# Differential attention: value products behind the scores of three units ahead, in ScalarE's banks and copied out by ScalarE

## The chip, the cores and the metric

The kernel runs on one core of a Trainium2 chip. Its time is the time of one execution on the device in microseconds (us). TensorE (PE) multiplies matrices and writes to eight banks of PSUM; VectorE (DVE) and ScalarE (ACT) read those banks; GpSimd (POOL) and SyncE (SP) issue transfers here. Each engine works through its own list of instructions in order, and the engines wait for each other by semaphores.

## The reference

Two transformer blocks on 512 tokens of width 1024, in float32. The change is in one part of the first block, the differential attention: four heads, each with two sets of queries and keys of width 64 and values of width 128.

```python
def one_block(args):
    qb, blk = args
    ...
    logits = jnp.einsum('bhqmd,bhmkd->bhmqk', qb, k_t).astype(f32) * scale
    logits = logits + bias[None, :, None]
    logits = jnp.where(allowed[None, None, None], logits, NEG_INF)
    probs = jax.nn.softmax(logits, axis=-1)
    attn = (probs[:, :, 0] - lam * probs[:, :, 1]).astype(v_t.dtype)
    return jnp.einsum('bhqk,bhkd->bhqd', attn, v_t)
...
o = rms_norm(from_blocks(o), out_g) * (1.0 - lam_init)
```

After it come the output projection (`w_out`), the residual, and the norm ahead of the feed-forward part.

## The kernel before

**Units and turns.** The differential attention is cut into 16 units: unit n is head n % 4 of the 128 tokens of group q = n // 4. A unit of group q has scores over (q + 1) * 128 keys. Every engine runs the loop `for n in DIFF_TURNS`, 25 turns, and each turn holds steps of several units and groups. What one engine does in turn n, in this order:

- **TensorE** (line 1055): the value product of unit n - 1, `diff_values` (q + 1 pairs of 128x128 tiles); the two score products of unit n + 3, `diff_scores`; in turns 0 and 4 eight matmuls of the conditioning (`modulation_sums`, line 849), in 2 and 6 one of its products (`modulation`, line 860); the turning (transposes, line 804) of unit n's weights, `diff_turns`. Then the steps of a group at fixed distances: in turn 4q + 6 `out_turned(q)`, in 4q + 11 `x_turned(q)`, and in turns 4q + 7 and 4q + 8 `out_product(q, 0)` and `out_product(q, 1)`, 128x1024 by 1024x512 each. The helper `product` records all these products as line 738.
- **VectorE** (line 1932): `diff_score(n + 2)` (line 1794, two reads of a bank with bias and row maximum), `diff_share(n)` (lines 1804 to 1807, which makes the difference of the two softmaxes and signals `p_ready`), `out_added` (line 1825), the copy `diff_out(n - 1)` (line 1799), and by group: `out_squares(q)` in turn 4q + 4 (lines 1811, 1812, 1601), `out_normal(q)` in 4q + 5 (lines 1598, 1818, 1819), `x_squares(q)` in 4q + 9 (line 1828), `x_normal(q)` in 4q + 10 (line 1834).
- **ScalarE** (line 2596): two exponentials of unit n (line 2603), the copy of unit n - 1's turned weights to `pT` (line 2515, the helper `copy_out`), in turn 4q + 7 the copy of the turned output rows to `yT`, the conditioning's copy in turns 0 and 4, and `root` (line 2504, a square root): in turn 4q + 5 for `out_squares(q)`, in 4q + 10 for `x_squares(q)`. `root` and the exponentials need different tables, so that a `root` brings two table loads: one before it, one before the exponential that follows.

**Banks.** The eight banks are two rings of four. VectorE empties banks 0 to 3, ScalarE banks 4 to 7, each in the order in which TensorE filled them. `bank` makes TensorE wait until the fill four before it in the same ring was copied out. Before the change VectorE's ring holds a value product and two scores in each turn, ScalarE's ring the turned weights.

**What waits for what.** The turning of unit n waits for `diff_share(n)`, that for the exponentials of n; the value product of n waits for the copy of n's turned weights (`mark["diff", "T", n]`); `out_normal(q)` waits for ScalarE's `root`; `out_turned(q)` for `out_normal(q)`; `x_turned(q)` for `x_normal(q)`. `pT` has two buffers, `diff_s` has three pairs.

```python
def group_at(n, after):

    q, rest = divmod(n - 4 - after, 4)
    return q if rest == 0 and 0 <= q < NT else None
```

Of the kernel before, what the change touches and what calls it, by code (L numbers as in the profile page):

```python
# [24 lines left out]
P = 128  # L25
# [151 lines left out]
def build(nc, t, out):  # L177
# [6 lines left out]
    with ExitStack() as ctx:  # L184
# [109 lines left out]
        diff_o = S1["v"]  # L294
# [241 lines left out]
        n = len(items)  # L536
# [160 lines left out]
        def _(pe):  # L697
# [4 lines left out]
            def bank(ring_name):  # L702

                n = done[ring_name]
                free = dve_free if ring_name == "dve" else act_free
                if n >= 4:
                    pe.wait_ge(free, n - 3)
                last_share = last_shares.pop(n % 4 + (0 if ring_name == "dve" else 4), None)
                if last_share is not None:
                    pe.wait_ge(*fast_bank_free(last_share))  # L710
                return banks[n % 4 + (0 if ring_name == "dve" else 4)]
# [310 lines left out]

            def diff_values(n):
                h, q = diff_units[n]
                b = bank("dve")
                pe.wait_ge(act_free, mark["diff", "T", n])
                full(product(b[:, 0:P], [(S1["pT"][:, n % 2, k, 0:P], S1["dv"][:, k, h * P:(h + 1) * P])
                                         for k in range(q + 1)]), "dve")
                mark["diff", "PV", n] = done["dve"]

            def out_turned(q):
                to_wait(tp_ready)
# [20 lines left out]
            diff_scores(1)  # L1053
            diff_scores(2)
            for n in DIFF_TURNS:
                if 1 <= n <= N_DIFF:
                    diff_values(n - 1)
                diff_scores(n + 3)
                if n in (0, 4):
                    modulation_sums(10 + n // 4)  # L1060
                if n in (2, 6):
                    modulation(10 + n // 4)
                if n < N_DIFF:
                    diff_turns(n)
                q = group_at(n, 2)
                if q is not None:
                    out_turned(q)
                q = group_at(n, 7)
                if q is not None:
                    if q == NT - 1:  # L1070
                        pe.wait_ge(dve_free, mark["ffn turned", 1])
                        fast_product(0, shares=(0,))
                    x_turned(q)
                for c in range(2):
                    q = group_at(n, 3 + c)
                    if q is not None:
                        out_product(q, c)
# [486 lines left out]
        def _(dve):  # L1564
# [229 lines left out]
                    V(dve.tensor_tensor_reduce(diff_s[j][:, 0:w], take()[:, 0:w], diff_bias[:, h, 384 - q * P:512],  # L1794
                                               -DIFF_QK ** -0.5, -BIG, ALU.add, ALU.min, neg_max[:, j:j + 1]), dve_free)

            def diff_out(n):
                h, q = diff_units[n]
                V(dve.tensor_copy(diff_o[:, q, h * P:(h + 1) * P], take()[:, 0:P]), dve_free)

            def diff_share(n):
                w, j = (diff_units[n][1] + 1) * P, 2 * (n % 3)
                wait_next(e_ready, 2)
# [3 lines left out]
                V(stt(s0, s0, row_sum[:, j:j + 1], s1, ALU.mult, ALU.subtract), p_ready)  # L1807

            def out_squares(q):
                v = diff_o[:, q, :].rearrange("p (g d) -> p g d", g=4)  # L1810
                V(tt(out_square, v, v, ALU.mult))
                V(dve.tensor_reduce(stat8[:, 0:DIFF_H], out_square, AX.X, ALU.add))
                scale_var(stat8[:, 0:DIFF_H], P, EPS, var_ready)
# [118 lines left out]
            for n in DIFF_TURNS:  # L1932
                if n + 2 < N_DIFF:
                    diff_score(n + 2)
                if n in (3, 7):
                    modulation(10 + n // 4)
                if n < N_DIFF:
                    diff_share(n)
                q = group_at(n, 8)
                if q is not None:  # L1940
                    turned_in(q, column("ffn_norm_g"), hT=ffn_hT)
                for c in range(2):
                    q = group_at(n, 4 + c)
                    if q is not None:
                        out_added(q, c)
                if 1 <= n <= N_DIFF:
                    diff_out(n - 1)
                for after, stage in ((1, out_normal), (0, out_squares), (6, x_normal), (5, x_squares)):
                    q = group_at(n, after)
                    if q is not None:  # L1950
                        stage(q)
                if n == N_DIFF + 5:
                    weight_sum(0, 0)
                if n == N_DIFF + 7:
                    weight_sum(0, 1)
# [526 lines left out]
        def _(act):  # L2482
# [31 lines left out]
            def copy_out(dst, src):  # L2514
                C(act.activation(dst, src, ACT.Copy), act_free)  # L2515
# [80 lines left out]
            for n in DIFF_TURNS:  # L2596
# [7 lines left out]
                                         accum_out=row_sum[:, j:j + 1]), e_ready)  # L2604
                if 1 <= n <= N_DIFF:
                    q = diff_units[n - 1][1]
                    if n >= 3:
                        act.wait_ge(dve_full, mark["diff", "PV", n - 3])
                    copy_out(S1["pT"][:, (n - 1) % 2, 0:q + 1, 0:P],
                             take()[:, 0:(q + 1) * P].rearrange("p (a b) -> p a b", a=q + 1))  # L2610
                q = group_at(n, 3)
                if q is not None:
                    copy_out(S1["yT"][:, 4:8, q * P:(q + 1) * P], take()[:, :].rearrange("p (a b) -> p a b", a=4))
                if n in (0, 4):
                    modulation_part(10 + n // 4)
                if group_at(n, 1) is not None:
# [421 lines left out]
```

## Time and profile before

| | |
|---|---|
| time, three runs | median 2320.02 us (2319.14 to 2322.25) |
| the profiled execution | 2320.72 us, span 2318.9 us |
| PE busy over the span | 2122.4 us (92%) |
| DVE busy | 1203.8 us (52%) |
| ACT busy | 439.4 us (19%) |
| differential attention, the 16 units with copies and norms | about 276 to 380 us of the span |

Times in the rows below count from the start of the span, in microseconds. In a timeline a row is a run of instructions of one line: its start, its length, what it is, how many, and in square brackets the idle time of the engine ahead of it and who ended it.

### The profile page before, as it was taken

What the parts mean: (1) busy time and instruction counts of PE and PEld (TensorE: products, weight loads), DVE (VectorE), ACT (ScalarE), POOL (GpSimd) and SP (SyncE); (2) the same over time, 40 slices, a digit from 0 to 9 for tenths busy, and PEclk for the clock granted to TensorE, in tenths of its full rate; (3) what the DMA queues carried; (4) which work ended last, traced back from release to release, by engine and by line L of the source; (5) the groups of instructions that cost most, each with busy time, mean ns of one, the idle gap of its engine ahead of it and who ended that gap; (6) DMA issues with size and microseconds to landing.
All of it is one profiled execution on the core that took longest, in us unless ns stands there. A gap on an engine that the chain in (4) does not pass through costs nothing.

```text
span 2318.9 us, 24664 instructions
## 1 busy us (share of the span) xinstructions
PE 2122.4 (92%) x9190; PEld 1351.5 (58%) x9190; DVE 1203.8 (52%) x2145; ACT 439.4 (19%) x901; POOL 125.1 (5%) x159
## 2 busy tenths in 40 slices
PE   7998788999999999998899999999996999999882
PEld 3444444888888844434688488888854333433330
DVE  4684563756676533287688357776446212121114
ACT  1124442100100010104311354510110000000003
POOL 0000000000000000000000044300000001010000
PEclk9998988999999999999999999999996999999986
DMA  7126510522222121221032100042443899999994
GB/s 276 37 86 241 190 48 1 153 75 74 72 100 100 66 86 73 73 73 37 1 109 73 37 1 1 2 145 73 146 184 130 367 427 426 427 426 426 427 423 183
DMA packets 97293, 364.71 MB, mean 157 GB/s; under 512 B 10396, under 2 KB 19281, under 8 KB 84625
## 3 DMA queue, kind: packets, MB, share of 16 engines
q1 hardware_dynamic: 86337, 340.62, 38.2%
q0 software_dynamic: 8720, 20.89, 2.4%
q8 instruction: 76, 1.25, 0.2%
q10 hardware_dynamic: 2112, 1.57, 0.2%
q14 instruction: 48, 0.39, 0.1%
HBM read 357.00 MB, written 17.57 MB: 162 GB/s over the span
## 4 chain that ended last, share of the span: by engine, by line
PE 74%; DVE 13%; DMA 7%; issue 3%; ACT 2%; SPq 0%; DVEq 0%; ACTq 0%; POOL 0%; POOLq 0%
PE bank L738 49%; PE bank L1527 8%; PE bank L1522 5%; DMA mem<-in_w_up 5%; PE bank L804 3%; PE bank L1217 2%; PE bank L974 2%; DVE mem L2103 1%; PE bank L849 1%; DVE mem L2102 1%; ACT mem L2515 1%; DMA mem<-in_w_in 1%; PE bank L1503 1%; DVE mem L1761 1%; PE bank L1157 1%
## 5 line engine op out<-in xcount | busy, mean ns | idle before, releaser
L738 PE MATMUL bank<-mem 128*128 128x256 f32 (+7 forms) x5024 | 1358.5, 432 | 31.8 <-ACT mem L2515 12.8
L738 PEld LDWEIGHTS bank<-mem 128*128 128x128 f32 (+2 forms) x5024 | 936.2, 193 | 404.8 <-issue 262.2
L1527 PE MATMUL bank<-mem 128*64 128x512 f32 x1248 | 287.3, 616 | 29.2 <-DMA mem<-in_w_up 16.6
L1527 PEld LDWEIGHTS bank<-mem 128*64 128x64 f32 x1248 | 93.1, 141 | 213.6 <-issue 202.2
L2515 ACT ACTIVATE mem<-bank 128x512 f32<-128x512 f32 (+5 forms) x269 | 136.8, 508 | 370.1 <-PE bank L738 153.1
L804 PE MATMUL bank<-mem 128*128 128x128 f32 (+1 forms) x708 | 118.8, 300 | 50.5 <-DVE mem L1761 24.6
L2451 DVE TENSOR_TENSOR mem<-mem,bank 128x512 f32<-128x512 f32 x19 | 13.1, 690 | 279.6 <-PE bank L1527 207.2
L804 PEld LDWEIGHTS bank<-mem 128*128 128x128 f32 (+1 forms) x708 | 88.1, 151 | 102.2 <-DVE mem L1761 37.6
L1522 PE MATMUL bank<-mem 128*128 128x512 f32 x288 | 132.3, 615 | 6.7 <-ACT mem L2797 4.1
L2628 ACT ACTIVATE mem<-bank 128x512 f32<-128x512 f32 (+1 forms) x62 | 36.3, 586 | 458.5 <-PE bank L738 456.8
L1522 PEld LDWEIGHTS bank<-mem 128*128 128x128 f32 x288 | 55.3, 196 | 78.7 <-issue 70.2
L2459 DVE TENSOR_TENSOR mem<-bank,mem 128x512 f32<-128x512 f32 x38 | 26.4, 693 | 106.1 <-PE bank L1527 71.3
L1217 PE MATMUL bank<-mem 128*128 128x128 f32 x512 | 64.1, 278 | 6.7 <-DVE mem L2243 5.0
L1847 DVE TENSOR_TENSOR mem<-mem 128x1024 f32<-128x1024 f32 (+2 forms) x31 | 36.4, 1175 | 62.5 <-PE bank L738 52.4
L1217 PEld LDWEIGHTS bank<-mem 128*128 128x128 f32 x512 | 59.9, 191 | 8.8 <-DVE mem L2243 6.0
L2795 ACT ACTIVATE mem<-bank 128x512 f32<-128x512 f32 x19 | 11.4, 599 | 262.7 <-PE bank L1527 191.4
L2165 DVE SCALAR_TENSOR_TENSOR mem<-mem 128x511 f32<-128x511 f32 (+2 forms) x72 | 54.1, 752 | 2.5
L2797 ACT ACTIVATE mem<-bank 128x512 f32<-128x512 f32 x19 | 11.4, 599 | 182.1 <-PE bank L1543 182.1
L974 PE MATMUL bank<-mem 128*64 128x512 f32 (+7 forms) x128 | 39.7, 454 | 3.1 <-ACT mem L2515 3.1
L1912 DVE TENSOR_TENSOR mem<-mem,bank 128x512 f32<-128x512 f32 (+1 forms) x30 | 20.2, 672 | 42.8 <-PE bank L738 42.4
L1892 DVE TENSOR_TENSOR mem<-mem,bank 128x512 f32<-128x512 f32 (+1 forms) x31 | 20.9, 673 | 39.3 <-PE bank L738 39.1
L1753 DVE CUSTOM_DVE_ANT_0 mem<-bank,mem 128x128 f32<-128x128 f32 (+1 forms) x64 | 31.5, 493 | 16.7 <-PE bank L738 14.8
(347 smaller groups left out, 1698.1 us busy)
## 6 DMA issues: line engine op xcount, KB each, us to landing
mem<-in_w_gate SPq DMA_DIRECT2D x37, 2048.0 KB, 23.3
mem<-in_w_up SPq DMA_DIRECT2D x37, 2048.0 KB, 23.5
mem<-in_w_down SPq DMA_DIRECT2D x36, 2048.0 KB, 22.5
mem<-in_w_in SPq DMA_DIRECT2D x18, 2048.0 KB, 7.7
mem<-in_w_ada SPq DMA_DIRECT2D x12, 2048.0 KB, 8.0
mem<-in_w_out SPq DMA_DIRECT2D x4, 2048.0 KB, 13.3
mem<-in_w_ple_gate SPq DMA_DIRECT2D x2, 2048.0 KB, 7.9
mem<-in_w_br_att SPq DMA_DIRECT2D x2, 2048.0 KB, 7.9
```

The source lines that it names most:

```text
L738: last = pe.matmul(o, l, r, start=(i == 0), stop=(i == len(pairs) - 1))
L804: last = pe.transpose(b[0:width, i * P:(i + 1) * P], s, ident)
L974: last = pe.matmul(o[:, k * P:SEQ], v_of(k, h), pT[:, h % nbuf, k, k * P:SEQ], start=(k == 0), stop=(k == NT - 1))
L1217: last = pe.matmul(b[:, h * P:(h + 1) * P], lhs(h), rhs(h), start=True, stop=True)
L1522: last_ = pe.matmul(o, lhs[:, k, :], ws[0][:, k, cols], start=(k == 0), stop=(k == kk - 1))
L1527: last_ = pe.matmul(o[here, :], lhs[:, k, here], w[:, k, cols], start=(k == 0), stop=(k == kk - 1))
L1753: V(dve.tensor_tensor_reduce(s[:, n % 3, 0:w], b[:, 0:w], bias_of(q), -scale, -BIG, ALU.add, ALU.min, neg_max[:, n % 4:n % 4 + 1]), dve_free)
L1847: V(tt(s1, feature_half(w, 0, 1), feature_half(w, 1, 1), ALU.add), w_summed)
L2165: V(stt(o, src[:, 0:SEQ - back], column("conv_w_2", (CONV2 - 1 - back) * 24 + m), o, ALU.mult, ALU.add), silu_in if back == CONV2 - 1 else ...
L2459: tt(yb[:, n % 2, at_], banks[5 + half][:, :], gate_rows[:, 1, at_], ALU.mult).then_inc(y_taken, 1)
L2515: C(act.activation(dst, src, ACT.Copy), act_free)
L2628: C(act.activation(dst[:, 0:cols], fast_bank(n, 3 * i)[:, 0:cols], ACT.Copy), fast_copied)
```

## The change

The value product of unit n - 1 goes to a bank of ScalarE's ring, not VectorE's. ScalarE copies it out, after the copies of turned weights and rows of the same turn and ahead of the conditioning's copy and `root`; VectorE's copy `diff_out` is gone. On TensorE the value product stands behind the score products of unit n + 3. `out_squares(q)` waits on ScalarE's copy of the group's last unit. ScalarE's wait for a free half of `pT` goes, since its own copy of the value product stands for it.

```diff
             def diff_values(n):
                 h, q = diff_units[n]
-                b = bank("dve")
+                b = bank("act")
                 pe.wait_ge(act_free, mark["diff", "T", n])
                 full(product(b[:, 0:P], [(S1["pT"][:, n % 2, k, 0:P], S1["dv"][:, k, h * P:(h + 1) * P])
-                                         for k in range(q + 1)]), "dve")
-                mark["diff", "PV", n] = done["dve"]
+                                         for k in range(q + 1)]), "act")
+                mark["diff", "PV", n] = done["act"]
...
             for n in DIFF_TURNS:
+                diff_scores(n + 3)
                 if 1 <= n <= N_DIFF:
                     diff_values(n - 1)
-                diff_scores(n + 3)
...
-            def diff_out(n):
-                h, q = diff_units[n]
-                V(dve.tensor_copy(diff_o[:, q, h * P:(h + 1) * P], take()[:, 0:P]), dve_free)
-
...
             def out_squares(q):
+                dve.wait_ge(act_free, mark["diff", "PV", 4 * q + 3])
                 v = diff_o[:, q, :].rearrange("p (g d) -> p g d", g=4)
...
-                if 1 <= n <= N_DIFF:
-                    diff_out(n - 1)
...
                 if 1 <= n <= N_DIFF:
                     q = diff_units[n - 1][1]
-                    if n >= 3:
-                        act.wait_ge(dve_full, mark["diff", "PV", n - 3])
                     copy_out(S1["pT"][:, (n - 1) % 2, 0:q + 1, 0:P],
                              take()[:, 0:(q + 1) * P].rearrange("p (a b) -> p a b", a=q + 1))
                 q = group_at(n, 3)
                 if q is not None:
                     copy_out(S1["yT"][:, 4:8, q * P:(q + 1) * P], take()[:, :].rearrange("p (a b) -> p a b", a=4))
+                if 1 <= n <= N_DIFF:
+                    h, q = diff_units[n - 1]
+                    copy_out(diff_o[:, q, h * P:(h + 1) * P], take()[:, 0:P])
                 if n in (0, 4):
                     modulation_part(10 + n // 4)
                 if group_at(n, 1) is not None:
```

On ScalarE, turns 9 and 10 (the exponentials of units 9 and 10, the copies of turned weights, the square roots) before:

```order
L2603 ACTIVATE mem<-mem 128x384 x2
L2515 ACTIVATE mem<-bank5 128x3x128
L2504 ACT_TABLE_LOAD
L2504 ACTIVATE mem<-mem 128x4
L2603 ACT_TABLE_LOAD
L2603 ACTIVATE mem<-mem 128x384 x2
L2515 ACTIVATE mem<-bank6 128x3x128
L2504 ACT_TABLE_LOAD
L2504 ACTIVATE mem<-mem 128x1
```

and after:

```order
L2598 ACTIVATE mem<-mem 128x384 x2
L2510 ACTIVATE mem<-bank5 128x3x128
L2510 ACTIVATE mem<-bank6 128x128
L2499 ACT_TABLE_LOAD
L2499 ACTIVATE mem<-mem 128x4
L2598 ACT_TABLE_LOAD
L2598 ACTIVATE mem<-mem 128x384 x2
L2510 ACTIVATE mem<-bank7 128x3x128
L2510 ACTIVATE mem<-bank4 128x128
L2499 ACT_TABLE_LOAD
L2499 ACTIVATE mem<-mem 128x1
```

The new rows are the two 128x128 copies from banks 6 and 4. Each stands between the copy of the turned weights and the table load of the square root.

On TensorE, turns 8 to 10 (x8 is an output product; 128x128 x3 of line 738 a value product with three tiles; two 128x512 a pair of scores; line 804 turned weights, and with x4 turned rows) before:

```order
L738 MATMUL bank1<-mem 128x512 x8
L738 MATMUL bank2<-mem 128x128 x3
L738 MATMUL bank3<-mem 128x512
L738 MATMUL bank0<-mem 128x512
L804 MATMUL bank6<-mem 128x128 x3
L738 MATMUL bank1<-mem 128x128 x3
L738 MATMUL bank2<-mem 128x512
L738 MATMUL bank3<-mem 128x512
L804 MATMUL bank7<-mem 128x128 x3
L804 MATMUL bank4<-mem 128x128 x4
```

and after:

```order
L738 MATMUL bank1<-mem 128x512 x8
L738 MATMUL bank2<-mem 128x512
L738 MATMUL bank3<-mem 128x512
L738 MATMUL bank6<-mem 128x128 x3
L804 MATMUL bank7<-mem 128x128 x3
L738 MATMUL bank0<-mem 128x512
L738 MATMUL bank1<-mem 128x512
L738 MATMUL bank4<-mem 128x128 x3
L804 MATMUL bank5<-mem 128x128 x3
L804 MATMUL bank6<-mem 128x128 x4
```

The value products moved from behind the output product and the turned weights to behind the pair of scores, and from banks 2 and 1 to banks 6 and 4. The output product of a turn still stands ahead of the value product of the next.

## Rows read from the trace of the kernel before

**Rows 1.** Page, part 4: the chain that ended last.
```profile
PE 74%; DVE 13%; DMA 7%; issue 3%; ACT 2%; SPq 0%; DVEq 0%; ACTq 0%; POOL 0%; POOLq 0%
```

**Rows 2.** Groups by line and form, 276 to 380 us.
```profile
L2504 ACT ACT_TABLE_LOAD x6 | 7.7, 1283 | 15.5 <-DVE mem L1601 15.5
...
L1799 DVE COPY mem<-bank 128x128 f32<-128x128 f32 x16 | 4.7, 293 | 2.7 <-PE bank L738 2.3
...
L2515 ACT ACTIVATE mem<-bank 128x128 f32<-128x128 f32 x4 | 1.1, 280 | 3.6 <-PE bank L804 3.6
```

**Rows 3.** Waits, 276 to 385 us: total, times, longest.
```profile
PE bank L738 <- ACT mem L2515: 10.2, 9, 2.2
```

**Rows 4.** Timeline of PE, turns 4 to 7.
```profile
293.76 2.77 PE L738 MATMUL bank<-mem 128*128 128x128 f32 x8 [2.19 <-ACT mem L2515]
...
298.24 2.78 PE L738 MATMUL bank<-mem 128*128 128x128 f32 x8 [1.09 <-ACT mem L2515]
...
299.37 1.65 PE L738 MATMUL bank<-mem 64*128 64x384 f32 x4
...
306.71 0.44 PE L804 MATMUL bank<-mem 128*128 128x128 f32 x2 [1.00 <-DVE mem L1807]
```

**Rows 5.** Timeline of ACT, turn 5 and 6.
```profile
293.63 1.28 ACT L2504 ACT_TABLE_LOAD   x1
...
296.45 0.51 ACT L2603 ACTIVATE mem<-mem 128x256 f32<-128x256 f32 x1
...
297.71 0.39 ACT L2515 ACTIVATE mem<-bank 128x256 f32<-128x256 f32 x1
```

**Rows 6.** Timeline of ACT, turns 9 to 11.
```profile
316.92 1.28 ACT L2504 ACT_TABLE_LOAD   x1 [0.51 <-DVE mem L1601]
...
327.01 1.28 ACT L2504 ACT_TABLE_LOAD   x1 [1.51 <-DVE mem L1601]
...
331.30 1.13 ACT L2515 ACTIVATE mem<-bank 128x384 f32<-128x384 f32 x2
```

**Rows 7.** Timeline of PE, turns 9 to 11.
```profile
324.34 0.55 PE L804 MATMUL bank<-mem 128*128 128x128 f32 x3
325.64 3.20 PE L738 MATMUL bank<-mem 128*128 128x128 f32 x10 [0.76 <-ACT mem L2515]
329.83 0.98 PE L804 MATMUL bank<-mem 128*128 128x128 f32 x7 [0.99 <-DVE mem L1807]
...
335.50 2.56 PE L804 MATMUL bank<-mem 128*128 128x128 f32 x11
```

**Rows 8.** Timeline of DVE, turns 9 and 10.
```profile
323.84 0.18 DVE L1598 RECIPROCAL mem<-mem 128x4 f32<-128x4 f32 x1
...
329.16 0.62 DVE L1807 SCALAR_TENSOR_TENSOR mem<-mem 128x384 f32<-128x384 f32 x1
```

**Rows 9.** Timeline of PE, turns 14 and 15.
```profile
356.33 1.13 PE L738 MATMUL bank<-mem 128*128 128x128 f32 x8 [0.86 <-ACT mem L2515]
360.18 1.97 PE L804 MATMUL bank<-mem 128*128 128x128 f32 x8 [2.73 <-DVE mem L1807]
363.88 2.05 PE L738 MATMUL bank<-mem 128*128 128x128 f32 x8 [1.73 <-ACT mem L2515]
365.72 2.77 PE L804 MATMUL bank<-mem 128*128 128x128 f32 x12
```

**Rows 10.** Timeline of ACT, turns 13 to 15.
```profile
347.99 1.28 ACT L2504 ACT_TABLE_LOAD   x1
...
358.63 1.28 ACT L2504 ACT_TABLE_LOAD   x1 [2.45 <-DVE mem L1601]
...
363.13 1.24 ACT L2515 ACTIVATE mem<-bank 128x512 f32<-128x512 f32 x2
```

**Rows 11.** Windows: length, busy time of each engine, then the granted clock (PEclk).
```profile
293.50:303.70 10.20, 8.85 (x25) 4.76 (x26) 5.37 (x15) 5.81 (x14) 0.00 (x0) 0.50 0.49 188
...
358.40:368.60 10.20, 6.69 (x29) 6.32 (x30) 5.30 (x13) 6.21 (x10) 0.00 (x0) 0.50 0.01 2
```

## The prediction

> **What bounds the kernel now.** I read the chain that ended last first: PE holds 74% of it [rows 1], so time is won where TensorE waits or runs at its lower clock. Then the waits of the stage: ahead of value products TensorE waited 10.2 us for ScalarE's copies, nine times, 2.2 us at most [rows 3]. That is what the scores could fill. Then the timelines of the three engines side by side. They show two kinds of turns. In turns 7 and 8, 11 and 12, 15 and 16 an output product of about 7 us stands on TensorE and VectorE and ScalarE have time in plenty. In the turns between, every engine waits for another in a ring: turned weights, ScalarE's copy, value product, and beside them the norms of a finished group, with ScalarE's square root. Last the windows for the clock: TensorE is granted half (1.2 GHz of 2.4) from 293.5 to 303.7 and 358.4 to 368.6 [rows 11], after waits of 2.19 us [rows 4] and of 0.86 us and more [rows 9].
>
> **The copies themselves.** 16 copies of 128x128 leave VectorE, 0.293 us each, and come to ScalarE at 0.280 us [rows 2]: 4.7 us against 4.5 us of busy time, no gain by itself. What decides is where the new copy stands in ScalarE's list. It waits for the value product of its unit, and behind it are queued the square root of the turn, the two exponentials of the next unit and the copy of the next turned weights; VectorE's norms and shares wait for these, and TensorE for the shares.
>
> **Turns 1 to 7, a gain.** A pair of scores fills the wait for ScalarE's copy of the turned weights, so up to turn 4 TensorE comes about 0.7 us sooner (an estimate: some 0.5 us in turn 4, where the scores now run while ScalarE copies, and 0.2 us brought along; the nine waits of [rows 3] are 1.1 us in the mean, but half of such a gain is lost again where the share of the turn is late). Then turn 5. The copy of unit 4's weights ended at 293.62 and its square root started at 293.63 [rows 5], while the value product had its start at 293.76 [rows 4]. With 0.7 us gained that product starts at 293.05; it takes some 0.8 us at the full clock, and ScalarE's copy another 0.1 + 0.28 us. The square root starts at 294.2, later by 0.6 us. From a square root to the end of the copy behind the next exponentials ScalarE's work is a solid row (293.63 to 298.10, [rows 5]), so value product 5 starts at 298.85, not 298.24 [rows 4]. But the scores of 1.65 us that followed it [rows 4] have been done before, so that turned weights 6 come 1.65 - 0.6 = 1.0 us sooner. From there to turned weights 7 at 306.71 [rows 4] VectorE's chain decides, as before. Term: **-1.0 us**. Bounds: if the shorter wait ahead of turn 5 keeps the full clock, what lies there takes about half as long, -2.5 us; if instead the longer wait ahead of value product 5 costs it further on, 0.
>
> **Turns 9 to 11, a loss.** Output product (0, 1) occupies TensorE until 322.5. Under it ScalarE did the square root of group 1 at 316.92 [rows 6]. Now the copy of unit 8 stands ahead of that root, and value product 8 stands behind the output product and the scores: it ends at about 324.4, just ahead of the turned weights of 324.34 [rows 7]. The root's table load starts at 324.4 + 0.1 + 0.28 = 324.8, later by 7.9 us, and nothing covers it. Load and root (1.28 + 0.2 us, [rows 2]) end at 326.3, VectorE's `out_normal(1)` starts there and not at 323.84, and so all of VectorE behind it, to the share of unit 10 that ended at 329.78 [rows 8], comes 2.5 us later: turned weights 10 at 332.3, not 329.83 [rows 7]. ScalarE goes on: from table load to the end of the next pair of exponentials took 331.30 - 327.01 = 4.29 us [rows 6], so the copy of weights 9 (0.49 us) ends at 324.8 + 4.3 + 0.5 = 329.6, value product 9 starts at 329.75 where it was 325.64 [rows 7]. Its wait is now over 3 us, so I take the lower clock: by the 1.13 us for two tiles (299.37 - 298.24, [rows 4]) three take 1.6 us. Its copy ends at 331.7, the second root (`x_squares(0)`) and its exponentials at 336.0, the copy at 336.5, value product 10 at 336.65 to 338.2. Behind it turned weights 11, at 335.50 before [rows 7]: **+2.7 us**. At the full clock the two value products are 0.7 to 0.8 us shorter each: +1.3 us.
>
> **Turns 13 to 15, the same once more.** The root of group 2 was at 347.99 [rows 10], under output product (1, 1). Now it follows the copy of unit 12, whose value product ends at 355.0. The copy ends at 355.4, root and exponentials at 359.9 (363.13 - 358.63 = 4.5 us, [rows 10]), the copy of weights 13 (0.60) at 360.5. Value product 13 starts at 360.65 instead of 356.33, takes 2.05 us at the lower clock (1.13 at the full one, [rows 9]), its copy ends at 363.1, root of `x_squares(1)` and exponentials of unit 15 at 367.6, the copy at 368.2, value product 14 at 368.35 instead of 363.88. Turned weights 15 follow 365.72 - 363.88 = 1.84 us behind [rows 9], at 370.2 instead of 365.72: **+4.5 us**. Both were at the lower clock in this stretch before [rows 11], and there is more waiting now, so I see no way back to the full clock; with it the term would be +2.6 us.
>
> **The clock behind.** Before, the full clock came back just as an output product began (303.7 and 368.6). I add **+0.7 us** for output products that now begin in a lower-clock stretch, an estimate: 1.4 us at half speed lose that in work. Bounds 0 and 3.
>
> **What costs nothing.** The wait of `out_squares(q)` for ScalarE's copy adds some 0.1 us and is under output products (turns 8, 12, 16) or behind a copy long done (turn 4). In turns 9 and 13 the exponentials of the unit come up to 7 us later than before, under the output product of turn 8 or 12, before VectorE's share is asked for; with that cover gone they would cost their 1.5 to 1.7 us. Turn 17's root has only `out_squares(3)` ahead and output product (2, 1) over it. TensorE's waits for banks get no longer: scores alone now reuse VectorE's banks, and four fills back in ScalarE's ring lie two units. Behind the stage TensorE's list of products starts later by what has been lost, as do the loads that it releases.
>
> **Sum:** -1.0 + 2.7 + 4.5 + 0.7 = +6.9 us. The profiled execution, 2320.72 us (its span 2318.9 us), would be 2327.6; it is 0.7 us above the median, and against that I predict 2320.0 + 6.9, about 2327 us. Three runs lay 3.1 us apart, and 0.2%, 4.6 us, is about what can be told from no change.
>
> **A page against the rows.** The root with its two table loads took 296.45 - 293.63 = 2.82 us here [rows 5]. The Trainium skill, ScalarE: Activation LUTs, section "What ACT_TABLE_LOAD costs", gives 1283 ns for the load, which the rows have too, but a drain on top, 2.66 us for every switch. By it the root that comes onto the path would cost 2.5 us more in each of the two places, and the sum would be about +12 us (2332). The rows show the load followed by the next instruction at once, so the sum goes by them.
>
> **Rivals.** (a) *No measurable change*: the same mechanism, with TensorE at its full clock in turns 9 to 15: -2.5 + 1.3 + 2.6 + 0 = +1.4 us, 2321.5, and up to +4.6 where only one stretch is spared. For it: idle times below 1.2 us left the clock alone at 325.64 [rows 7]. Against it: the new waits are 3 and 5 us. Chance 0.30. (b) *Faster*: the roots are not late enough to matter, and the scores' cover is all that is left: -1.0 to -2.5 us in turns 1 to 7, 0.76 and 0.86 us of waits filled or kept [rows 7, 9], and less lower clock, some -5 us, 2315. It decides at the place of value product 8: VectorE wants the root at 323.84, 1.5 us behind its start, so its copy would have to end by 322.3, and that is still inside the output product. Chance 0.07. (c) *The new ring in every turn*: value product, copy, exponentials, copy of weights, on ScalarE's side without a gap: in group 3 about 1.1 to 2.05 + 0.4 + 1.7 + 0.7 = 4 to 5 us a turn. Where turns were shorter (1 to 6) it would cost up to 1 us each, +12 us in all, 2332. Against it: these turns have narrow units with 1 us of exponentials. Chance 0.08. My forecast: 0.55.
>
> **Numbers.** Slower by over 0.2% takes (c) and most of the forecast, 0.62; within 0.2% takes (a) and a little of the forecast, 0.31; faster 0.07. The range, 2320.5 to 2332, leaves out (b) and the far end of (c).
>
> **What would show it.** In the profile after: ScalarE's table load of turn 9 behind a 128x128 copy and behind output product (0, 1), 7 to 8 us later against its surroundings; VectorE idle ahead of the reciprocal of `out_normal(1)` and `(2)`, for ScalarE, some 2.5 and 1.5 us; waits of TensorE of 3 to 5 us ahead of value products 9 and 13, and turned weights 15 about 6 us later than 365.72; turned weights 7 ahead of 306.71. Wrong it would be if the lower-clock stretches end sooner or fewer come, or if the gain of the first seven turns is several times as large.

## The result, and the profile after

The changed kernel took 2334.11 us in the median of six runs (2328.49 to 2335.99), the kernel before beside it 2321.22 us (six runs, 2319.14 to 2324.14): ratio 1.0055 [1.0042, 1.0067]. It is slower by 12.9 us, and 2334 lies outside my range of 2320.5 to 2332. A second set of runs (e1 below) gave 10.6 us. One execution of the experiments (the profiled one of e10) ran at a granted clock of 0.55 and took 3702 us; its time and trace are left out.

The profiled execution took 2335.23 us, span 2333.4. Page of the kernel after, parts 1 and 4 (answers to [rows 1]):

```profile
PE 2132.6 (91%) x9190; PEld 1358.1 (58%) x9190; DVE 1198.9 (51%) x2129; ACT 443.8 (19%) x917; POOL 124.4 (5%) x159
...
PE 74%; DVE 12%; DMA 7%; issue 3%; ACT 2%; SPq 0%; DVEq 0%; ACTq 0%; POOL 0%; POOLq 0%
```

The copies moved as forecast (VectorE 4.9 us less, ScalarE 4.4 us more), and the chain hardly differs. But PE is busy for 2132.6 us, not 2122.4: the same 9190 matmuls took 10 us longer. That is the clock, not a wait, and not all of it is the change's: this execution had 13 us more at the lower clock ahead of the stage, where nothing was changed, and 11 us more behind it. In a second trace of the same kernel (e1) PE is busy for 2120.4 us. A page alone can't say what the change did.

Now the place in question. Waits of the kernel after, 282 to 391 us (total, times, longest), answering to [rows 3]:

```profile
ACT mem L2510 <- PE bank L738: 50.4, 16, 8.4
...
PE bank L738 <- ACT mem L2510: 21.2, 9, 5.2
...
DVE mem L1598 <- ACT mem L2499: 11.3, 5, 3.1
```

TensorE's nine waits for ScalarE's copies grew from 10.2 us to 21.2 (longest 5.2, was 2.2). ScalarE waits sixteen times for a value product, up to 8.4 us, and VectorE's reciprocal 3.1 us for ScalarE's root. The timelines of the kernel after show how. ScalarE, turns 9, 10 and 13 ([rows 6, 10] before):

```profile
331.59 0.28 ACT L2510 ACTIVATE mem<-bank 128x128 f32<-128x128 f32 x1 [6.85 <-PE bank L738]
331.89 1.28 ACT L2499 ACT_TABLE_LOAD   x1
...
334.70 0.62 ACT L2598 ACTIVATE mem<-mem 128x384 f32<-128x384 f32 x1
...
343.12 1.13 ACT L2510 ACTIVATE mem<-bank 128x384 f32<-128x384 f32 x2
...
363.46 0.28 ACT L2510 ACTIVATE mem<-bank 128x128 f32<-128x128 f32 x1 [5.60 <-PE bank L738]
363.76 1.28 ACT L2499 ACT_TABLE_LOAD   x1
```

VectorE, turn 9 ([rows 8] before):

```profile
333.49 0.18 DVE L1598 RECIPROCAL mem<-mem 128x4 f32<-128x4 f32 x1 [3.12 <-ACT mem L2499]
...
338.80 0.62 DVE L1803 SCALAR_TENSOR_TENSOR mem<-mem 128x384 f32<-128x384 f32 x1
```

TensorE, turns 5 to 7, 9 to 12 and 14 to 15 ([rows 4, 7, 9] before):

```profile
302.04 0.68 PE L738 MATMUL bank<-mem 128*128 128x128 f32 x4 [1.35 <-ACT mem L2510]
...
307.72 0.68 PE L738 MATMUL bank<-mem 128*128 128x128 f32 x4 [3.67 <-ACT mem L2510]
...
313.55 0.44 PE L804 MATMUL bank<-mem 128*128 128x128 f32 x2 [0.51 <-DVE mem L1803]
...
331.75 1.13 PE L738 MATMUL bank<-mem 64*128 64x512 f32 x4
336.82 1.62 PE L738 MATMUL bank<-mem 128*128 128x128 f32 x6 [3.94 <-ACT mem L2510]
339.48 1.76 PE L804 MATMUL bank<-mem 128*128 128x128 f32 x7 [1.04 <-DVE mem L1803]
...
344.59 1.42 PE L804 MATMUL bank<-mem 128*128 128x128 f32 x11
...
346.11 9.04 PE L738 MATMUL bank<-mem 128*128 128x512 f32 x26
...
369.01 2.05 PE L738 MATMUL bank<-mem 128*128 128x128 f32 x8 [5.21 <-ACT mem L2510]
...
376.70 1.96 PE L738 MATMUL bank<-mem 128*128 128x128 f32 x8 [3.94 <-ACT mem L2510]
378.45 2.34 PE L804 MATMUL bank<-mem 128*128 128x128 f32 x12
```

The signs that the prediction named are there: ScalarE sat 6.85 us in front of the copy of value product 8, its table load right behind; then VectorE's 3.12 us, and 3.94 and 5.21 us ahead of value products 9 and 13. Counted from each kernel's first score read, the table load of turn 9 came at 331.89 - 280.55 = 51.3 us, before at 316.92 - 274.54 = 42.4: 9.0 us later, where 7 to 8 were forecast. One sign is missing: turned weights 7 came no sooner (they stand under "Why" below).

**Three segments.** Starts differ between executions, so I cut each trace at the same four events: the first score read of the stage (VectorE, line 1794), the last addition of an output product (`out_added(3, 1)`), the first matmul of the experts (TensorE, line 1522 in both kernels), and the end. "Half clock" is the time at the lower granted level, 1.2 GHz. These are differences of start times in the timelines, in us:

```
run                 start   stage  half clock | behind  half clock | rest
before, 1st        274.5   130.9    34.1      | 1388.4    63.4     | 525.0
before, 2nd (e5)   275.9   130.9    34.1      | 1387.7    62.8     | 522.0
before, 3rd (e6)   275.2   130.7    30.7      | 1387.4    62.4     | 522.5
before, 4th (e17)  272.8   133.4    38.2      | 1388.0    63.3     | 521.2
before, 5th (e18)  280.0   130.7    30.7      | 1388.3    63.3     | 525.2
after, 1st         280.6   136.8    34.8      | 1392.6    74.6     | 523.5
after, 2nd (e1)    278.0   136.8    34.8      | 1393.0    75.1     | 525.2
after, 3rd (e11)   274.9   137.7    37.5      | 1392.1    74.0     | 524.4
```

The stage costs 5.9 us (twice; 6.8 once), near the +6.9 of the sum. Another 4 to 5 us come in 1390 us of program behind the stage that the change does not touch. The start is a drift of executions: it varies over 7 us in the kernel before alone, so the 6 us of it in the first pair of profiles can't be put down to the change (means 275.7 us in five traces of before, 277.8 in three of after).

Windows of both kernels over the part behind (length, busy time of PE, PEld, DVE, ACT, POOL, granted clock, DMA share, GB/s). After, then one of its stretches at half clock:

```profile
417.40:1810.00 1392.60, 1329.07 (x6131) 997.72 (x6129) 862.48 (x1416) 271.82 (x555) 77.84 (x109) 0.97 0.23 77
...
1141.40:1148.20 6.80, 5.38 (x12) 2.90 (x10) 0.12 (x1) 0.60 (x1) 0.00 (x0) 0.50 0.00 0
```

Before, then its stretch at the same distance from the stage's end (1141.40 - 417.36 = 1129.50 - 405.45 = 724.0 us):

```profile
405.40:1794.00 1388.60, 1325.09 (x6131) 994.67 (x6129) 862.71 (x1416) 271.85 (x555) 77.96 (x109) 0.98 0.23 78
...
1129.50:1136.30 6.80, 4.71 (x20) 3.32 (x21) 2.68 (x4) 1.09 (x2) 0.00 (x0) 1.00 0.00 0
```

The same 6131 matmuls; DVE and ACT are busy alike to 0.3 us, PE 4.0 us longer. The eight matmuls of line 974 that stand in the second stretch, the kernel after:

```profile
1143.02 4.61 PE L974 MATMUL bank<-mem 128*128 128x512 f32 x8 [0.84 <-ACT mem L2510]
```

and the kernel before:

```profile
1131.39 2.39 PE L974 MATMUL bank<-mem 128*128 128x512 f32 x8 [0.84 <-ACT mem L2515]
```

The wait ahead of them is 0.84 us in both; only the clock differs.

### The profile page after: what moved, and what is told of

It reads as the page before. It is cut to its first block, busy times and chain, and to the rows that moved or that the text cites. A ratio compares the mean times of both kernels' runs of the same rounds, so it can differ in the third digit from the quotient of the medians.

```text
span 2333.4 us, 24668 instructions
## 1 busy us (share of the span) xinstructions
PE 2132.6 (91%) x9190; PEld 1358.1 (58%) x9190; DVE 1198.9 (51%) x2129; ACT 443.8 (19%) x917; POOL 124.4 (5%) x159
## 4 chain that ended last, share of the span: by engine, by line
PE 74%; DVE 12%; DMA 7%; issue 3%; ACT 2%; SPq 0%; DVEq 0%; ACTq 0%; POOL 0%; POOLq 0%
PE bank L738 49%; PE bank L1527 8%; PE bank L1522 5%; DMA mem<-in_w_up 5%; PE bank L804 3%; PE bank L1217 2%; PE bank L974 2%; PE bank L849 1%; DVE mem L2098 1%; DVE mem L2097 1%; ACT mem L2510 1%; PE bank L1503 1%; DMA mem<-in_w_in 1%; PE bank L1157 1%; DVE mem L1761 1%
## 5 line engine op out<-in xcount | busy, mean ns | idle before, releaser
L738 PE MATMUL bank<-mem 128*128 128x256 f32 (+7 forms) x5024 | 1362.9, 433 | 42.4 <-ACT mem L2510 23.8
L2510 ACT ACTIVATE mem<-bank 128x512 f32<-128x512 f32 (+6 forms) x285 | 141.2, 496 | 391.0 <-PE bank L738 202.7
L974 PE MATMUL bank<-mem 128*64 128x512 f32 (+7 forms) x128 | 42.4, 479 | 3.1 <-ACT mem L2510 3.1
L1909 DVE TENSOR_TENSOR mem<-mem,bank 128x512 f32<-128x512 f32 (+1 forms) x30 | 20.2, 672 | 45.2 <-PE bank L738 44.8
L1598 DVE RECIPROCAL mem<-mem 128x8 f32<-128x8 f32 (+2 forms) x39 | 7.2, 184 | 66.0 <-ACT mem L2499 59.8
## 6 DMA issues: line engine op xcount, KB each, us to landing
mem<-in_w_up SPq DMA_DIRECT2D x37, 2048.0 KB, 24.6
```

The lines of the kernel that those rows point to most:

```text
L738: last = pe.matmul(o, l, r, start=(i == 0), stop=(i == len(pairs) - 1))
L974: last = pe.matmul(o[:, k * P:SEQ], v_of(k, h), pT[:, h % nbuf, k, k * P:SEQ], start=(k == 0), stop=(k == NT - 1))
```

## The experiments

**e1, e5, e6, e11, e17, e18: both kernels again.** No edit.

> The changed kernel once more, unaltered. Its first profile began the stage (first score product of differential attention) at 279.6 us against 273.6 before, 6.0 us late ahead of anything that the change touches, and was 5.9 us longer inside the stage and 2.6 us behind it. Theory M: only what lies inside the stage is the change's (square roots behind the new copy), the rest is the drift of one execution, so that the stage is again 5 to 7 us longer while its start lies anywhere from 273 to 280; time +6 to +13 us. Rival N: the changed program is slower outside the stage too, and the start is at 279 to 280 again, time +12 to +14 us.

> The kernel before, unaltered, for a second trace of it. The five traces of changed kernels began the stage 1.0 to 6.0 us later than the one trace of before, although the program ahead of it is the same, and TensorE's lower-clock stretches lay elsewhere. Drift theory: this trace begins the stage 1 to 6 us later than 274.5 us too, and its stage (first score to the last output product) may be a few us off 130.9. Theory N (the change slows the program outside the stage): it begins at 274.5 again. Time within 0.2% of before either way.

> The kernel before, unaltered, for a third trace, with the same two expectations as for the second: the drift theory has the start of the stage and the places of the lower clock vary between the traces of one kernel, theory N has them as in the first.

> The changed kernel, unaltered, for a third trace: the stage 5.9 us longer than before as in both others (6.9 predicted for it), the start between 274 and 281 us.

> The kernel before, unaltered, a fourth trace. If the start of the stage is the drift of an execution, at least one of this and the next begins it later than 276.5 us; if an altered program begins later by itself, both lie at 274.5 to 276. The stage 130.7 to 130.9 us, the stretch from its last output product to the experts 1387.4 to 1388.4 us, unless the later start brings the other pattern of the clock (1391.6 us and more).

> The kernel before, unaltered, a fifth trace, with the same expectations as the fourth.

Measured: after 2333.41 (six runs) against 2322.79, ratio 1.0044 [1.0028, 1.0060], and one run of 2330.94; before 2323.02 against 2323.95 (ratio 1.0008 [0.9991, 1.0026]), and single runs of 2317.57, 2317.21 and 2326.04. The traces gave the table above. Stage and part behind repeat within about 1 us for each kernel, except one stage of 133.4; the start does not repeat. The fifth trace of before began its stage at 280.0 us and still had 1388.3 us behind it: a late start does not bring the longer part behind.

**e2, e8: the roots ahead of the copy.** The cause of the loss should be ScalarE's order. e2 puts both `root`s ahead of the new copy, e8 only that of the output norm.

```diff
+                if group_at(n, 1) is not None:
+                    root(stat8[:, 0:DIFF_H])
+                q = group_at(n, 6)
+                if q is not None:
+                    root(stat[:, q:q + 1])
                 if 1 <= n <= N_DIFF:
                     h, q = diff_units[n - 1]
                     copy_out(diff_o[:, q, h * P:(h + 1) * P], take()[:, 0:P])
                 if n in (0, 4):
                     modulation_part(10 + n // 4)
-                if group_at(n, 1) is not None:
-                    root(stat8[:, 0:DIFF_H])
-                q = group_at(n, 6)
-                if q is not None:
-                    root(stat[:, q:q + 1])
```

(e8 leaves the second of the two where it was.)

> The changed kernel with one edit: in each turn ScalarE does its square roots ahead of the copy of the value product, not behind it. Only the next turn's exponentials and copy of turned weights still wait behind the copy. Theory M: VectorE's norms of groups 1 and 2 have their root under the output product again, the stage is 1 to 3 us longer than before in place of 5.9, time +1 to +4 us. Rival (the copy's wait itself, ahead of the exponentials, is the cost): the stage stays 5 to 7 us longer, time +6 or more. Rival N: start of the stage at 279 to 280, 6 us on top of either.

> The changed kernel with only the square root of the output norm (turns 5, 9, 13, 17) ahead of the copy; the square root of the feed-forward norm (turns 10, 14) stays behind it. With both ahead the stage went from +5.9 to -0.9 us. If the output norm's root is what came late, this one has most of that: stage 0 to +2 us, time +2 to +5 us. If the feed-forward norm's root carries it, the stage stays at +4 us or more.

Measured, e2: 2326.86 (twelve runs), ratio 1.0016 [1.0005, 1.0027], stage 129.97, 6.8 us less than after. ScalarE:

```profile
329.06 0.28 ACT L2510 ACTIVATE mem<-bank 128x128 f32<-128x128 f32 x1 [5.33 <-PE bank L738]
329.36 1.28 ACT L2598 ACT_TABLE_LOAD   x1
```

VectorE and TensorE of e2:

```profile
327.87 0.18 DVE L1598 RECIPROCAL mem<-mem 128x4 f32<-128x4 f32 x1
```

```profile
332.77 0.91 PE L738 MATMUL bank<-mem 128*128 128x128 f32 x6 [2.42 <-ACT mem L2510]
```

The copy still waits 5.33 us, but the root is no longer behind it: the reciprocal has no wait, and value product 9 waits 2.42 us, not 3.94. e8: 2329.43, ratio 1.0025 [1.0012, 1.0039], stage 134.52, 2.3 us less. So moving the output norm's root gave 2.3 us, about a third of the 6.8, and moving the feed-forward norm's root as well the other two thirds (the second move alone was not run). The order on ScalarE is the cause in the stage; what of the 6.8 us is wait and what is clock is not separated (24.6 us of e2's stage are at half clock, 34.8 of after's). e2's stage had been expected 1 to 3 us longer than before and came out 0.9 us shorter; e8's, 3.6 us longer, is nearer to the 4 us that had been expected if the feed-forward norm's root carried the loss than to the 0 to 2 us of the other case. Yet e2, with the shorter stage, stays slower than before: behind it are 1393.2 us.

**e3, e12: the copy a turn later.** ScalarE copies value product n - 2 right behind the exponentials of unit n, when it is long done; nothing has to wait for it.

```diff
+                if 2 <= n <= N_DIFF + 1:
+                    h, q = diff_units[n - 2]
+                    copy_out(diff_o[:, q, h * P:(h + 1) * P], take()[:, 0:P])
+                if n == 0 or n == 5:
+                    modulation_part(10 + n // 5)
                 if 1 <= n <= N_DIFF:
                     q = diff_units[n - 1][1]
                     copy_out(S1["pT"][:, (n - 1) % 2, 0:q + 1, 0:P],
...
-                if 1 <= n <= N_DIFF:
-                    h, q = diff_units[n - 1]
-                    copy_out(diff_o[:, q, h * P:(h + 1) * P], take()[:, 0:P])
-                if n in (0, 4):
-                    modulation_part(10 + n // 4)
```

> The changed kernel with ScalarE's copy of a value product one turn later, behind the next unit's exponentials (and the conditioning's copy behind it, as the ring wants), so that neither root nor exponentials ever wait for a value product. Theory M: nothing of the loss is left, the scores still fill TensorE's waits: the stage is 1 to 4 us shorter than before, time -1 to -4 us. Rival (ScalarE's 16 more copies, or the value product behind the scores, cost in themselves): the stage is 2 us or more longer than before. Rival N: time 6 us above what the stage says.

> The version with ScalarE's copy one turn later once more, for a second trace and more times: its stage 4 to 5 us shorter than before again; if it beats both kernels, time -1 to -4 us with an interval below 1.

Measured: 2321.05, ratio 0.9993 [0.9981, 1.0005], and 2319.92, ratio 0.9988 [0.9979, 0.9998], twelve runs each. The stage takes 126.2 and 124.2 us, 4.7 and 6.7 less than before. TensorE in e3:

```profile
326.83 2.00 PE L738 MATMUL bank<-mem 64*128 64x512 f32 x10
331.47 0.98 PE L804 MATMUL bank<-mem 128*128 128x128 f32 x7 [2.65 <-DVE mem L1803]
...
333.89 0.91 PE L738 MATMUL bank<-mem 128*128 128x128 f32 x6 [0.38 <-ACT mem L2510]
```

The ten matmuls are the scores and value product 8 together, and value product 9 waits 0.38 us. This is what the cover of the scores can give. Behind it come 1393.9 and 1393.3 us, and most is lost again: e3's interval includes no change, and e12's ends just below it.

**e4, e7: the value product in its old place,** ahead of the scores, in the changed kernel (e4) and in e3's (e7).

```diff
             for n in DIFF_TURNS:
-                diff_scores(n + 3)
                 if 1 <= n <= N_DIFF:
                     diff_values(n - 1)
+                diff_scores(n + 3)
```

> The changed kernel with the value product ahead of the scores again, as before; ScalarE's ring and copy stay. Theory M: each value product ends one pair of scores (0.6 to 1.1 us) sooner and with it the roots behind it, but the scores no longer fill waits: stage 4 to 6 us longer than before, time +4 to +8 us. Rival (the place behind the scores is what costs): stage within 1.5 us of before, time within 2 us.

> ScalarE's copy one turn later, behind the next exponentials, and the value product ahead of the scores as before. Theory R (the place behind the scores was worth 7.4 us under the late wait, 5.9 against 13.3 us of stage, because it alone gives TensorE work while ScalarE waits): with nothing waiting on ScalarE it is worth what the filled waits are, 2 to 5 us; the stage is 0 to 3 us shorter than before, time 0 to -2 us. Rival (the place is worth 7 us whatever stands behind the copy): stage 2 us or more longer than before.

Measured: e4 2337.30, ratio 1.0060 [1.0038, 1.0082], stage 144.25, 7.4 us more than after and 13.3 more than before, far more than I expected of it. e7 2326.02, ratio 1.0006 [0.9994, 1.0018], stage 127.97, 1.8 and 3.7 us above e3 and e12. TensorE in e4, where I had expected a short wait ahead of a value product:

```profile
335.47 3.50 PE L738 MATMUL bank<-mem 128*128 128x128 f32 x10 [3.79 <-ACT mem L2510]
```

e7's stage is 2.9 us shorter than before, as expected, but its time is not: 1391.6 us lie behind it. So the place behind the scores is a gain in both, largest while the copy makes everybody late; what makes the stage slow is where the copy stands. And e4 has 1388.4 us behind its stage, the value of before, though its program there is the changed kernel's.

**e9, e10, e13 to e16: a delay at the stage's end.** Is it the moment at which the stage ends that costs the 4 to 5 us behind? The kernel before, with N unused multiplies on VectorE in `out_normal(3)`; nothing else changes.

```diff
             def out_normal(q):
                 v = diff_o[:, q, :].rearrange("p (g d) -> p g d", g=4)
                 invert(stat8[:, 0:DIFF_H])
+                if q == NT - 1:
+                    for _ in range(8):
+                        V(tt(out_square, v, v, ALU.mult))
```

> The kernel before with nothing of the change, but with eight further multiplies of 128x512 (0.73 us each, 5.8 us in all) on VectorE in turn 17, ahead of the last group's output norm, where TensorE waits for it. Their result is used by nobody. It shifts all that follows by about what the change costs inside the stage. Theory P (what was lost outside the stage is TensorE's clock, which falls at other places once the same program runs at another time): behind the last output product 2 us or more are lost beside the three traces of before, time +9 to +14 us. Rival (the loss outside comes from the changed program itself): behind it within 1 us of them, time +6 to +8 us.

> The same with four multiplies, 2.9 us. Theory P: behind the last output product the loss is some value between -1 and +5 us that need not be the one with eight, time +3 to +8 us. Rival: within 1 us of before behind it, time +3 to +4 us.

> The kernel before with one further multiply (0.73 us) in turn 17, its result unused. If the moment decides, lower-clock time between 900 and 1900 us may be anything from 58 to 75 us and the time from the last output product to the experts goes with it (0 at 58 to 65, +3 to +5 at 72 to 75). If the changed program decides, it is 58 to 65 and within 1 us of before.

> The same with two multiplies, 1.5 us. If the moment decides, at least one of the four delays has 70 us or more of lower clock behind the stage and 3 us or more of extra time; if the changed program decides, none has.

> The same with three multiplies, 2.2 us, and the same two expectations.

> The same with six multiplies, 4.4 us, and the same two expectations.

The eight multiplies in e9 and the wait behind them, VectorE and TensorE:

```profile
392.90 5.79 DVE L1820 TENSOR_TENSOR mem<-mem 128x512 f32<-128x512 f32 x8
```

```profile
400.20 1.12 PE L804 MATMUL bank<-mem 128*128 128x128 f32 x4 [8.35 <-DVE mem L1822]
```

Measured: e9 2332.74, ratio 1.0044 [1.0031, 1.0057]; e10 2330.71 (six runs), ratio 1.0035 [1.0023, 1.0047], no trace; e13, e14, e15, e16 one run each, 2325.34, 2326.49, 2328.96, 2335.42 beside 2319.51. The part behind, by the traces, with the runs of the other kernels:

```
run                        stage  | behind  half clock
before + 1 multiply (e13)  131.2  | 1391.8    73.9
before + 2 (e14)           136.5  | 1388.7    62.7
before + 3 (e15)           136.3  | 1388.4    63.1
before + 6 (e16)           138.0  | 1391.6    73.9
before + 8 (e9)            140.3  | 1388.7    59.7
value product's place (e4) 144.3  | 1388.4    63.2
roots first (e2)           130.0  | 1393.2    75.2
one root first (e8)        134.5  | 1391.7    73.9
late copy (e3)             126.2  | 1393.9    75.6
late copy again (e12)      124.2  | 1393.3    75.4
late, old place (e7)       128.0  | 1391.6    73.7
```

The same work takes either 1387.4 to 1388.7 us with 60 to 63 us at half clock, or 1391.6 to 1393.9 us with 74 to 76; there is nothing between. One multiply of 0.7 us, which lengthened the stage by 0.3 us, brought the kernel before into the second group; two, three and eight left it in the first, though they lengthened the stage by 5 to 9 us; with six it is in the second again. In e9 the part behind came out as the rival of its expectation had it (within 1 us of before); the 2 us or more that Theory P wanted came in e13 and e16 alone. So neither the move of the copy nor a longer stage makes the 4 us. In the window of e13 (columns as above):

```profile
1137.00:1141.00 4.00, 3.71 (x8) 2.02 (x6) 0.19 (x1) 0.00 (x0) 0.00 (x0) 0.50 0.00 0
```

e13 is the kernel before, and it has the stretch at half clock that the kernel before lacks (there 1129.5 to 1136.3 was at 1.00) and the kernel after has.

The moment at which the stage ends does not sort the traces either. Counted from the start of the span, stages end at 405.5, 405.9 and 406.7 us (before, first group) and at 405.8 (e7, second); at 410.7 (before, e18, first) and at 410.3 (e13) and 410.5 (e8, second); at 416.9 (e15, first) and at 417.4 (e16, second). What repeats is the kernel: before fell in the first group five times of five, after in the second three times of three, the late copy (e3, e12) in the second twice. Programs that differ by one unused multiply can differ in the group.

One thing ahead of 724 us also goes by the kernel. In all five traces of before VectorE starts a reciprocal, about 679 us behind the stage's end, after an idle 0.37 us that no wait in the profile explains, and TensorE waits 0.41 us for what follows. In the other 14 traces the two idle times are at most 0.04 and 0.12 us, in e13 too. Before:

```profile
1084.13 0.16 DVE L1760 RECIPROCAL mem<-mem 128x1 f32<-128x1 f32 x1 [0.37 <-DVE mem L1753]
```

```profile
1084.87 0.66 PE L804 MATMUL bank<-mem 128*128 128x128 f32 x4 [0.41 <-DVE mem L1761]
```

and e13:

```profile
1088.35 0.16 DVE L1760 RECIPROCAL mem<-mem 128x1 f32<-128x1 f32 x1
```

```profile
1089.09 0.66 PE L804 MATMUL bank<-mem 128*128 128x128 f32 x4
```

Ahead of 724 us it is the only one of TensorE's idle times that separates the five traces of before from the ten of the second group by 0.25 us or more; across it the ten gain about 0.35 us. That this pause decides on the clock at 724 us is not shown.

## Why the prediction was right and wrong

**The copies themselves, and ScalarE's queue: right.** 4.9 us left VectorE and 4.4 came to ScalarE, and e2 shows that the order on ScalarE is the cause of the stage's loss. VectorE's waits for the root were 3.1 and 2.1 us, forecast some 2.5 and 1.5.

**The stage: +5.9 us where the sum had +6.9, in part by luck.** All times are from each trace's first score read, in us; the forecast column adds up the terms of the sum.

```
                     forecast | before  after  measured
turned weights 7       -1.0   |  32.2    33.0   +0.8
turned weights 11      +1.7   |  61.0    64.0   +3.1
turned weights 15      +6.2   |  91.2    97.9   +6.7
end of the stage       +6.9   | 130.9   136.8   +5.9
```

Term by term: +0.8 for -1.0, +2.3 for +2.7, +3.6 for +4.5, -0.8 for +0.7. The mechanism of the two losses was right and each a little smaller than forecast; the gain ahead of them did not come, and the clock term had the wrong sign. These misses cancel but for 1 us.

- *Turns 1 to 7, -1.0: the gain did not come.* Turned weights 7 started at 313.55 - 280.55 = 33.0 us, before at 306.71 - 274.54 = 32.2 [rows 4]: +0.8, and against three of the other traces of before (e5, e6, e18) it is +0.1 to +0.3. The scores did gain up to turn 5, as I had it. A second trace of before (e5) has value product 4 at 298.21 - 275.87 = 22.3 us, the kernel after at 302.04 - 280.55 = 21.5, 0.85 us sooner. Then it went: value product 5 waited 3.67 us for ScalarE, and the scores no longer behind it were worth 0.9 us at the full clock, where I had taken 1.65 us from a row at the lower one. [Rows 4] lay in a lower-clock stretch that other executions of the same kernel have elsewhere. TensorE in e5, where the product and the scores together take 1.53 us:

```profile
298.21 2.78 PE L738 MATMUL bank<-mem 128*128 128x128 f32 x8 [2.19 <-ACT mem L2515]
...
302.69 1.53 PE L738 MATMUL bank<-mem 128*128 128x128 f32 x8 [1.09 <-ACT mem L2515]
...
308.75 0.44 PE L804 MATMUL bank<-mem 128*128 128x128 f32 x2 [0.99 <-DVE mem L1807]
```

- *Turns 9 to 11, +2.7 forecast, +2.3 measured, and 13 to 15, +4.5 and +3.6.* Turned weights 11 (the row of eleven on line 804) started at 344.59 - 280.55 = 64.0, before at 335.50 - 274.54 = 61.0 [rows 7]. Those eleven took 1.42 us at the full clock, before 2.56 us, so that the row of 26 matmuls with output product (1, 0) began only 2.2 us later than before (346.11 - 280.55 = 65.6, and 337.89 - 274.54 = 63.4 by the row below). Turned weights 15 started at 378.45 - 280.55 = 97.9 against 365.72 - 274.54 = 91.2 [rows 9]. Value product 13 was at the lower clock as forecast (2.05 us), value product 9 too (1.62 us, forecast 1.6); value product 10, forecast 1.5 to 1.6 us as well, was back at the full clock (0.91 us). The kernel after, then before:

```profile
343.76 0.91 PE L738 MATMUL bank<-mem 128*128 128x128 f32 x6 [0.75 <-ACT mem L2510]
```

```profile
337.89 8.77 PE L738 MATMUL bank<-mem 128*128 128x512 f32 x26
```

- *The clock behind turn 15, +0.7: it was -0.8, outside its bounds of 0 and 3.* From turned weights 15 to the end of the stage the kernel before had 368.6 - 365.7 = 2.9 us left of one stretch at half clock and another from 385.7 to 392.5; the kernel after had 376.8 to 380.2, of which 1.8 us lay there, and 400.7 to 404.1.

**The step that failed is the sentence "Behind the stage TensorE's list of products starts later by what has been lost".** It took 1390 us of unchanged work for a constant. They cost 4 to 5 us more (1392.1 to 1393.0 against 1387.4 to 1388.4), 11 to 13 us more of them at half clock. With the 5.9 to 6.8 us of the stage this makes 10 to 12 us, against 12.9 and 10.6 in the medians; the rest is in the start and end, which vary by more than that. With the part behind as in the first group, the same stage would have given about 2321.2 + 5.9 = 2327 us (an estimate), inside the range, and e4 shows that a program with ScalarE's copy can be in that group. What the delays show is that this amount is not the work of the moved copy: the kernel before pays it too after one extra multiply. It repeats with each kernel and does not go by the moment at which the stage ends. What is not shown is why these kernels fall into two groups. Up to 670 us behind the stage all five traces of the kernel before and all ten of the second group have their stretches at half clock at the same distance from the stage's end, within 0.6 us; they part at 724 us, where the ten have one of 6.8 us more (after: 1141.4 - 417.4 = 724.0), and another of 3.4 us at 1024 us. The other four of the first group (e4, e9, e14, e15) have other arrangements, with a stretch of 10.2 us at 721 to 722 us, and nearly the same total. Why the clock parts there stays open, and with it whether the pause of 0.37 us has a part in it.

**The page against the rows.** By the Trainium skill's ScalarE: Activation LUTs, section "What ACT_TABLE_LOAD costs", the sum would have been about +12 us (an estimate), close to the measured total, but for the wrong reason. In the kernel after, table load, root, second table load took 334.70 - 331.89 = 2.81 us; the load of 1.28 us agrees with the page, the drain that it adds per switch is not in the rows, and the stage lost 5.9 us, not 12.

**The rivals.** (a), the full clock in turns 9 to 15, is out: value products 9, 13 and 14 were at half clock, and only 10 was spared. (b), faster, is not this kernel; with the copy where nothing waits for it (e3, e12) the stage is 4.7 to 6.7 us shorter, and the time 0.07% and 0.12% shorter. (c), a longer turn everywhere, did not come: up to turn 7 the loss is below 1 us. Its 2332 us lay nearest to the measured 2334, by chance: the stage lost 5.9 us, not 12.

## What to carry to other kernels

A copy that is cheap by its busy time (0.28 us) is as dear as what stands behind it in its engine's list: put it where its input is long done (here a turn later, e12), and the same move of work turns from 1.0055 to 0.9993 and 0.9988 in two sets of runs (e12's [0.9979, 0.9998]), no loss and at most a small gain. Below about half a per cent, do not carry a gain or loss of one stage one to one to the end of a long kernel: trace both kernels two or three times, cut them at common events, and compare the time at half clock in the part that was not changed. Repeats of one kernel are not enough for that, since here each kept its own pattern; a variant with one unused instruction (e13) showed the other. Take durations for a sum from a row at the clock that the new schedule will have there, not from the one profiled execution's.

## What the runs showed that I had not expected

- The unchanged 1390 us behind the stage have two lengths, about 1388 and about 1392.5 us, with 60 to 63 and 74 to 76 us at half clock; one unused multiply of 0.7 us changed the one into the other, and each kernel that was traced again kept its own.
- The stage of the kernel before varied from 130.7 to 133.4 us over five executions, with 31 to 38 us at half clock, and its start from 272.8 to 280.0 us.
- Eight multiplies of 5.79 us in all lengthened the stage by 9.4 us, and two of 1.5 us by 5.6 us (of which up to 2.7 us can be the stage's own variation): in e9 TensorE, which waited 8.35 us for VectorE, was at half clock from 394.3 to 407.9, in that wait and behind it (its four matmuls of turned rows took 1.12 us).
